# Two value banks in turn, and importance products moved to the end of a step, in a one-core decoder layer

## The chip, the cores and the metric

The kernel runs on one core of one Trainium2 chip. It is written engine by engine: TensorE does matrix products and full transposes and writes only to PSUM (8 banks of 512 float32 per partition), VectorE and ScalarE work element by element and read PSUM, GpSimd and SyncE do little here. The engines are held together by semaphores. The metric is the time on the device for one execution, in microseconds (us).

## The reference, cut to what matters

One decoder layer on 1024 tokens of width 1024: an input projection, then attention and a state-space mixer side by side, an output projection, and a mixture of experts. The change touches attention alone. Eight query heads share two key/value heads (four per group, `GQA`). For each block of 128 queries there are three branches, and their outputs are added with gates:

```python
p_cmp = masked_softmax(s, dist >= 0)                 # over 63 compressed keys
o_cmp = einsum('bkgqn,bnkd->bqkgd', p_cmp, v_cmp)
imp = einsum('bkgqn,nj->bkqj', p_cmp, ov)            # importance of 16 blocks of 64 keys
score = where(forced, FORCE_SCORE, where(valid, imp, -1.0))
_, idx = top_k(score, 8)                             # blocks that the selected branch may see
...                                                  # o_slc: softmax over the chosen blocks
...                                                  # o_win: softmax over the last 256 keys
o = gc[..., 0:1] * o_cmp + gc[..., 1:2] * o_slc + gc[..., 2:3] * o_win
```

Importance is needed only for query blocks 4 to 7: earlier blocks see at most 8 key blocks, so all are chosen.

## The kernel before

Attention (`attend`, L952) works through 24 groups, each a pair of branch and query block c: (CMP, 0), (WIN, 0), and then for each c (CMP, c+1), (WIN, c+1), (SEL, c). A group is cut into slots of some of the four heads per key/value head (`score_slots`): 46 slots (J) in all, one per group for CMP, two for most of WIN and for SEL 1 to 3, four for SEL 4 to 7. A slot is in flight over several steps, and each engine runs its own loop over steps j:

- TensorE (from L1223): scores of slot j; compressed values of slot j-2 (L1163, the products at L1170 for importance and L1175 for values) or values of slot j-2 (L1188), by kind; the turn of a finished group (L1198); transposes of the weights of slot j-1 (L1152), four 128 x 128 blocks to a PSUM bank, so one to four banks a slot; at times the transpose of a selection (L1205).
- ScalarE (from L1273): the copy of a finished group's values out of PSUM (`copy_values`, L1263), copies of the transposed weights of slot j-1 (L1270), exponentials of slot j (L1257).
- VectorE (from L1402): scores plus distance with the maximum (L1323), then `read_values` (L1327): the gates (L1337 to L1339), and either compressed values read straight from PSUM (L1343) and importance (L1347, then the release at L1350), or the turned values (L1353) and their addition (L1355); then the steps of the selection (L1365 to L1380) and the transposes of later queries (L293).

Values of WIN and SEL come out of the products with head width on the partitions and queries along the row; ScalarE copies them to SBUF and TensorE turns them with four transposes, so that VectorE can read them per query.

PSUM: scores use banks 0 to 3. All groups put their values into bank 6 (`O_BANK`). Transposes, importance, turned values, selections and one small product share banks 4, 5 and 7 in a fixed ring (`bank_users`, from L1059): the n-th user takes the bank of user n-3 and waits until that one has been read. Before the first products of a group, `bank_is_free` (L1155) waits for the reader of the group before: VectorE's read if it was CMP, ScalarE's copy if not. Each engine's order is fixed by its loop; an engine that waits holds up all that follows on it.

Of the kernel before, what the change touches and what calls it, by code (L numbers as in the profile page):

```python
# [24 lines left out]
P = 128  # L25
# [4 lines left out]
HD = 64  # L30
# [96 lines left out]
class Names:  # L127
# [11 lines left out]
    def sem(self, name):  # L139
        return self.stack.enter_context(self.nc.semaphore(name))  # L140
# [811 lines left out]
def attend(nc, N, M, A, C, out, next_tensor, next_vector):  # L952
# [20 lines left out]
    score_rows = M["score_rows"].rearrange("p (a c j) -> p a c j", a=2, c=NT)  # L973
    neg, coef, *den = (M["att_small"][:, i * 24:(i + 1) * 24].rearrange("p (b h) -> p b h", b=3) for i in range(4))
    o_T = M["misc"][:, 2048:3072].rearrange("p (b n) -> p b n", b=2)
    O_BANK, TURN_BANKS = 6, (4, 5, 7)

    gates_exp = sem("gates_exp")
    q_rows = M["q_rows"]
    scores_full, max_ready, exp_done = sem("scores_full"), sem("maxima_ready"), sem("exp_done")  # L980
    wT_full, wT_done = sem("weights_transposed"), sem("weightsT_copied")
    pv_done, o_read = sem("slot_values_done"), sem("values_read")
    oT_copied, o_turned, imp_read = sem("valuesT_copied"), sem("values_turned"), sem("importance_read")
    sel_ready, sel_full, sel_rows = sem("selection_ready"), sem("selection_transposed"), sem("selection_rows")
    prep_full, prep_steps = sem("ssd_constants_full"), sem("ssd_constants_steps")
    z_full, z_copied = sem("z_full"), sem("z_copied")
# [55 lines left out]
    def weightsT(j, k):  # L1042

        at = ((4096, 6144, 4608, 6656) if (J - 1 - j) % 2 == 0 else (0, 1024, 2048, 3072))[k]
        return M["big_u"][:, at:at + BANK]
# [10 lines left out]
    turns_before = lambda gi: sum(1 for x in turned if x < gi)  # L1056
    turn_at = {last_slot[groups[gi]] + 3: gi for gi in turned}
    imp_at = {last_slot[CMP, c] + 2: c for c in sel_count}
    bank_users, copy_use, sel_use, imp_use, turn_use, prep_use = [], [], {}, {}, {}, None  # L1059
    for j in range(J + 3):  # L1060
        if j in imp_at:
            imp_use[imp_at[j]] = len(bank_users)
            bank_users.append((imp_read, sel_count[imp_at[j]]))
        if j in turn_at:
            while j == J + 2 and TURN_BANKS[len(bank_users) % 3] != 7:
                bank_users.append(bank_users[-3])
            turn_use[turn_at[j]] = len(bank_users)
            bank_users.append((o_read, turn_at[j] + 1))
        if 1 <= j <= J:
            for k in range(len(banks_of(j - 1))):  # L1070
                copy_use.append(len(bank_users))
                bank_users.append((wT_done, len(copy_use)))
        if j in sel_at:
            sel_use[sel_at[j]] = len(bank_users)
            bank_users.append((sel_rows, sel_count[sel_at[j]]))
        if j == prep_at:
            prep_use = len(bank_users)
            bank_users.append((dt_sem, 7))
    bank_of = lambda use: TURN_BANKS[use % 3]

    queries_at = {0: [(1, 0), (1, 1)], 1: [(1, 2), (1, 3)]}
    for c in range(1, NT - 1):
# [26 lines left out]
    def tensor(pe):  # L1109
        def transpose_bank(use):  # L1110

            if use >= 3:
                pe.wait_ge(*bank_users[use - 3])
            return bank_of(use)

        def scores(j):
# [37 lines left out]

        def bank_is_free(gi):  # L1155

            if groups[gi - 1][0] == CMP:
                pe.wait_ge(o_read, gi)
            else:
                pe.wait_ge(oT_copied, turns_before(gi))  # L1160

        def compressed_values(j):

            gi, br, c, pairs = slots[j]
            pe.wait_ge(wT_done, copies_before[j + 1])
            rows = [weightsT(j, 0)[:, r * P:(r + 1) * P] for r in pairs]
            if c in sel_count:
                bank = transpose_bank(imp_use[c])
                for r in pairs:
                    nc.tensor.matmul(ps[:, bank, r * NG * N_BLK:(r + 1) * NG * N_BLK], rows[r], v_cmp[:, NG * HD:CMP_V],  # L1170
                                     start=True, stop=True)
            if gi >= 1:
                bank_is_free(gi)
            for r in pairs:
                last = nc.tensor.matmul(ps[:, O_BANK, r * P:(r + 1) * P], rows[r], v_cmp[:, 0:NG * HD], start=True, stop=True)  # L1175
            last.then_inc(pv_done, 1)

        def values(j):

            gi, br, c, pairs = slots[j]  # L1180
            if j == first_slot[br, c]:
                bank_is_free(gi)
            pe.wait_ge(wT_done, copies_before[j + 1])
            blocks, m = key_blocks(br, c), len(pairs)
            for b, blk in enumerate(blocks):
                for g in range(NG):
                    x = (b * NG + g) * m
                    last = nc.tensor.matmul(ps[g * HD:(g + 1) * HD, O_BANK, pairs[0] * P:(pairs[-1] + 1) * P],  # L1188
                                            vals[br][:, blk, g, 0:HD], weightsT(j, x // 4)[:, x % 4 * P:(x % 4 + m) * P],
                                            start=(b == 0), stop=(b == len(blocks) - 1))  # L1190
            last.then_inc(pv_done, 1)

        def turn_values(gi):

            pe.wait_ge(oT_copied, turns_before(gi) + 1)
            bank = transpose_bank(turn_use[gi])
            for r in range(GQ):
                last = nc.tensor.transpose(ps[:, bank, r * P:(r + 1) * P], o_T[:, turns_before(gi) % 2, r * P:(r + 1) * P],  # L1198
                                           ident[:, :])
            last.then_inc(o_turned, 1)  # L1200

# [21 lines left out]
        for j in range(J + 3):  # L1223
            n_t = len(banks_of(j - 1)) if 1 <= j <= J else 0
            if j < J:
                scores(j)
            if 2 <= j < J + 2 and slots[j - 2][1] == CMP:
                compressed_values(j - 2)
            if j in piece_at:
                z_pieces(piece_at[j][0], piece_at[j][1])  # L1230
            if j == J + 1:
                next_tensor(pe)
            if 2 <= j < J + 2 and slots[j - 2][1] != CMP:
                values(j - 2)
            if j in turn_at:
                turn_values(turn_at[j])
            if j in piece_at:
                z_pieces(piece_at[j][1], piece_at[j][2])
            for k in range(n_t):
                transposes(j - 1, k)  # L1240
            if j in sel_at:
                selection(sel_at[j])
            if j == prep_at:
                ssd_constants()

    def scalar(act):
# [13 lines left out]

        def copy_values(gi):
            act.wait_ge(pv_done, last_slot[groups[gi]] + 1)
            nc.scalar.activation(o_T[:, turns_before(gi) % 2, :], ps[:, O_BANK, :], ACT.Copy).then_inc(oT_copied, 1)  # L1263

        def copy_weights(j):
            for k, blocks in enumerate(banks_of(j)):
# [23 lines left out]
    def vector(dve):  # L1290
# [36 lines left out]
        def read_values(gi):  # L1327

            br, c = groups[gi]
            bank = O_BANK if br == CMP else bank_of(turn_use[gi])  # L1330
            O = ps[:, bank, :].rearrange("p (r g d) -> p g r d", r=GQ, g=NG)
            dst, tmp = by_head(o_att[:, c, :]), by_head(M["o_tmp"])
            gate_at = {CMP: 0, SEL: 1, WIN: 2}[br]
            d, f = (v[:, br, :] for v in (den[c % 2], coef))
            dve.wait_ge(exp_done, last_slot[br, c] + 1)
            if br == CMP:
                o.done(nc.vector.tensor_scalar(d, d, 1.0e-30, None, ALU.max))  # L1337
            o.done(nc.vector.reciprocal(d, d))
            o.done(nc.vector.tensor_tensor(f, d, sg[:, c, :, gate_at], ALU.mult))  # L1339
            fb = f.rearrange("p (g r) -> p g r", g=NG).unsqueeze(3).broadcast_to([P, NG, GQ, HD])  # L1340
            if br == CMP:
                dve.wait_ge(pv_done, last_slot[br, c] + 1)
                o.done(nc.vector.tensor_tensor(dst, O, fb, ALU.mult))  # L1343
                dve.sem_inc(o_read, 1)
                if c in sel_count:
                    imp_all = ps[:, bank_of(imp_use[c]), 0:GQ * NG * N_BLK].rearrange("p (r g j) -> p g r j", r=GQ, g=NG)
                    o.done(nc.vector.tensor_tensor(imp_h.rearrange("p (g r j) -> p g r j", g=NG, r=GQ), imp_all,  # L1347
                                                   d.rearrange("p (g r) -> p g r", g=NG).unsqueeze(3)
                                                   .broadcast_to([P, NG, GQ, N_BLK]), ALU.mult))
                    dve.sem_inc(imp_read, 1)  # L1350
            else:
                dve.wait_ge(o_turned, turns_before(gi) + 1)
                nc.vector.tensor_tensor(tmp, O, fb, ALU.mult).then_inc(o_read, 1)  # L1353
                dve.wait_ge(o_read, gi + 1)
                o.done(nc.vector.tensor_tensor(o_att[:, c, :], o_att[:, c, :], M["o_tmp"], ALU.add))  # L1355
                if gi == len(groups) - 1:
                    dve.sem_inc(rows_done, 1)

        def select(c, step):

# [39 lines left out]
        for gi, (br, c) in enumerate(groups):  # L1400
            read_at.setdefault(last_slot[br, c] + (2 if br == CMP else 3), []).append(gi)
        for j in range(J + 3):  # L1402
            if j < J:
                scores_with_distance(j)
            if j == 0:
# [1282 lines left out]
```

## Time and profile before

| | us |
|---|---|
| median of 3 runs | 1082.05 (1080.61 to 1083.12) |
| the profiled execution, its own time | 1081.66 |
| its span, first to last instruction | 1079.9 |
| TensorE busy | 1011.3 |
| VectorE busy | 645.8 |
| ScalarE busy | 345.6 |
| attention | about 305 to 605 us of the span |

Durations are those of one profiled execution. In the views PE is TensorE's matmul, PEld its weight load, DVE VectorE, ACT ScalarE. A row of the timeline merges neighbouring instructions of one line: start, duration of the row, engine, line, what it writes and reads, how many, and in brackets how long the engine was idle before and who released it. A row of a few matmuls ends a little later than the next row starts, as matmuls are pipelined. PEclk is the granted clock of TensorE: 1.00 is 2.4 GHz, 0.5 is 1.2 GHz, and a stretch between the two mixes them.

### The profile page before, as it was taken

To read this page: it belongs to the slowest core of one execution; us is meant where nothing else is said; L and a number is where in the kernel's file an instruction comes from. 1 tells how busy PE (TensorE), PEld (TensorE's weight loads), DVE (VectorE), ACT (ScalarE), POOL (GpSimd) and SP (SyncE) were. 2 spreads that over 40 slices of the span, in tenths; PEclk is the share of its full clock that TensorE was granted. 3 is DMA by queue.
4 is the path that set the end of the run, shared out by engine and by line. 5 is a ranking of instruction groups with operands and counts; after the bars stand their busy time and mean duration, and the time that the engine had idled before them with its cause. 6 is when DMAs were issued, how large, how long until landed. Compare 5 with 4: busy or idle time off the path is not lost.

```text
span 1079.9 us, 14099 instructions
## 1 busy us (share of the span) xinstructions
PE 1011.3 (94%) x4535; PEld 573.7 (53%) x4536; DVE 645.8 (60%) x1630; ACT 345.6 (32%) x974; POOL 175.4 (16%) x214
## 2 busy tenths in 40 slices
PE   8999999999998787878799899999989999999997
PEld 5544574444554554555556886555574444444443
DVE  3421222555254675676654598775577788887885
ACT  3311121121144665666666673322121000000000
POOL 0020131111000400000000210111012333333333
PEclk9999999999999988999999999999999999999999
DMA  7220042003000200000000501422749969999332
GB/s 267 90 71 0 1 81 78 21 17 103 1 1 1 79 1 1 1 1 2 1 1 2 188 9 34 157 77 99 252 152 319 351 228 332 327 385 350 126 115 95
DMA packets 73688, 119.26 MB, mean 110 GB/s; under 512 B 13888, under 2 KB 53152, under 8 KB 73632
## 3 DMA queue, kind: packets, MB, share of 16 engines
q1 hardware_dynamic: 62544, 87.59, 24.1%
q0 software_dynamic: 11088, 30.95, 8.1%
q8 instruction: 32, 0.52, 0.2%
q14 instruction: 24, 0.20, 0.1%
HBM read 105.41 MB, written 21.50 MB: 118 GB/s over the span
## 4 chain that ended last, share of the span: by engine, by line
PE 50%; ACT 10%; DVE 9%; issue 2%; DMA 0%; POOL 0%; DVEq 0%; POOLq 0%; ACTq 0%
PE ps L1858 16%; PE ps L1868 8%; ACT ring_gate_up L1257 5%; PE ps L2181 5%; PE ps L1188 4%; PE ps L1152 4%; PE ps L1218 3%; PE ps L1141 3%; ACT big_u L1270 3%; PE ps L2191 2%; PE ps L2212 1%; PE ps L1175 1%; PE ps L1198 1%; DVE big_u L2400 1%; ACT misc L1263 1%
## 5 line engine op out<-in xcount | busy, mean ns | idle before, releaser
L1672 DVE STREAM_TRANSPOSE big_w<-big_w 32x256 f32<-32x256 f32 x384 | 167.3, 436 | 28.3 <-DMA big_w<-hn_dram,misc 22.1
L1858 PE MATMUL ps<-ring_gate_up,big_w 128*128 (+1 forms) x400 | 179.8, 592 | 0.3 <-ACT big_w L1912 0.3
L519 PE MATMUL ps<-big_w,big_u 128*128 128x512 f32 (+1 forms) x448 | 174.6, 544 | 0.8 <-DVE big_u L795 0.8
L519 PEld LDWEIGHTS ps<-big_w,big_u 128*128 128x128 f32 x448 | 83.9, 192 | 77.3 <-issue 70.7
L1858 PEld LDWEIGHTS ps<-ring_gate_up,big_w 128*128 128x128 f32 x400 | 74.0, 190 | 83.8 <-issue 83.7
L1257 ACT ACTIVATE ring_gate_up<-ring_gate_up,big_w 128x64 f32<-128x64 f32 (+8 forms) x192 | 106.1, 562 | 1.1 <-DVE big_w L1323 1.1
L1323 DVE CUSTOM_DVE_ANT_0 ring_gate_up<-ps,ring_down 128x384 f32<-128x384 f32 (+7 forms) x128 | 73.9, 629 | 50.1 <-PE ps L1141 49.6
L1270 ACT ACTIVATE big_u<-ps 128x512 f32<-128x512 f32 (+1 forms) x126 | 66.4, 584 | 114.0 <-PE ps L1152 113.7
L1868 PE MATMUL ps<-ring_down,big_w 128*128 x200 | 90.0, 593 | 0.6 <-ACT big_w L1902 0.6
L1152 PE MATMUL ps<-ident,ring_gate_up 128*128 128x128 f32 x488 | 68.1, 287 | 17.1 <-DVEq L1350 12.7
L1188 PE MATMUL ps<-big_u,ring_down 128*64 128x128 f32 (+2 forms) x656 | 60.8, 331 | 17.7 <-ACT misc L1263 16.1
L1152 PEld LDWEIGHTS ps<-ident,ring_gate_up 128*128 128x128 f32 x488 | 57.1, 148 | 30.9 <-DVEq L1350 13.6
L1494 POOL TENSOR_SCALAR big_w<-big_w,vecT 128x1024 f32<-128x1024 f32 x8 | 23.2, 2907 | 251.1 <-DMA big_w<-in_w_out 251.1
L1141 PE MATMUL ps<-ring_down,misc 64*128 64x384 f32 (+3 forms) x320 | 63.1, 504 | 0.7 <-DVE big_w L1323 0.7
L1868 PEld LDWEIGHTS ps<-ring_down,big_w 128*128 128x128 f32 x200 | 37.9, 190 | 48.1 <-issue 48.1
L1902 ACT ACTIVATE big_w<-ps 128x256 f32<-128x256 f32 x25 | 9.6, 384 | 161.9 <-PE ps L1832 161.9
L1188 PEld LDWEIGHTS ps<-big_u,ring_down 128*64 128x64 f32 x656 | 38.8, 140 | 41.6 <-ACT misc L1263 19.1
L840 DVE TENSOR_REDUCE small<-ring_gate_up 128x2 f32<-128x128 f32 x16 | 4.6, 286 | 62.6 <-ACT ring_gate_up L659 42.4
L1795 POOL DMA_INDIRECT out<-big_u,misc x25 | 25.1, 1003 | 95.4 <-DVE big_u L1936 93.6
L293 DVE STREAM_TRANSPOSE misc<-ring_gate_up 32x128 f32<-32x128 f32 x128 | 38.7, 302 | 2.7 <-DVE ring_down L1343 0.2
L874 DVE TENSOR_TENSOR ring_gate_up<-ps,ring_gate_up 128x512 f32<-128x512 f32 x12 | 8.3, 693 | 52.9 <-PE ps L551 52.5
L1257 ACT ACTIVATION_READ_ACCUMULATOR ring_gate_up<-ring_gate_up,big_w 128x1 f32 x192 | 37.8, 197 | 0.0
(394 smaller groups left out, 1429.5 us busy)
## 6 DMA issues: line engine op xcount, KB each, us to landing
ring_gate_up<-in_w_gate SPq DMA_DIRECT2D x16, 1024.0 KB, 8.4
ring_gate_up<-in_w_up SPq DMA_DIRECT2D x16, 1024.0 KB, 12.4
ring_down<-in_w_down SPq DMA_DIRECT2D x16, 1024.0 KB, 14.3
misc<-in_x SPq DMA_DIRECT2D x16, 512.0 KB, 3.5
big_w<-in_w_in SPq DMA_DIRECT2D x6, 1024.0 KB, 7.0
big_w<-in_w_out SPq DMA_DIRECT2D x8, 512.0 KB, 5.1
hn_dram<-big_u SPq DMA_DIRECT2D x8, 512.0 KB, 2.6
out<-ring_gate_up SPq DMA_DIRECT2D x8, 512.0 KB, 3.9
```

What stands on the lines that cost most here:

```text
L293: last = nc.vector.transpose(dst[j * 32:(j + 1) * 32, :, i * 32:(i + 1) * 32], src[i * 32:(i + 1) * 32, :, d:d + 32])
L519: last = nc.tensor.matmul(ps[:, b, 0:width], uT[:, k, c * P:(c + 1) * P], wbuf[:, n % 2, k, 0:width], start=(k == 0), stop=(k == KD - 1))
L1141: last = nc.tensor.matmul(place(j, i, g)[:, at:at + w], Q[rows, c % 4, r * P:(r + 1) * P], rhs, start=not chosen, stop=True)
L1152: last = nc.tensor.transpose(ps[:, bank, i * P:(i + 1) * P], w_rows[:, at:at + P], ident[:, :])
L1188: last = nc.tensor.matmul(ps[g * HD:(g + 1) * HD, O_BANK, pairs[0] * P:(pairs[-1] + 1) * P], vals[br][:, blk, g, 0:HD], weightsT(j, x // 4 ...
L1257: last = nc.scalar.activation(w, w, ACT.Exp, bias=neg[:, br, h:h + 1], scale=-1.0, accum_out=den[c % 2][:, br, h:h + 1])
L1270: nc.scalar.activation(weightsT(j, k)[:, 0:w], ps[:, bank_of(copy_use[use]), 0:w], ACT.Copy).then_inc(wT_done, 1)
L1323: nc.vector.tensor_tensor_reduce(out=weights(j, i, g), in0=place(j, i, g), in1=table, scale=-SLOPES[h], scalar=1.0e20, op0=ALU.add, op1=AL ...
L1672: last = nc.vector.transpose(dst[j * 32:(j + 1) * 32, :, i * 32:(i + 1) * 32], src[i * 32:(i + 1) * 32, :, j * 32:(j + 1) * 32])
L1858: last = nc.tensor.matmul(ps[:, 2 + b, :], xT[:, b, k, :], ring_gu[:, bass.ds(at + k * 2 * D_EXP, BANK)], start=(k == 0), stop=(k == KD - 1))
L1868: last = nc.tensor.matmul(ps[:, 4 + 2 * b + half, :], hT[:, b, f, :], ring_d[:, bass.ds(at + f * D + half * BANK, BANK)], start=(f == 0), ...
L2181: last = nc.tensor.matmul(ps[:, bank, :], left[:, k, :], right[:, k, :], start=(k == 0 and starts), stop=(k == 3), skip_group_check=True)
```

## The change

Groups put their values into banks 6 and 7 in turn, by their number. A group may start when the group two before it has been read. The turned values go back into the bank that they came from. The ring for transposes, importance and selection has two banks, 4 and 5, and a user waits for the one two before. The importance products leave `compressed_values`, where they stood ahead of the compressed values, and come after the transposes of the same step; VectorE reads them at the start of the next step, ahead of its scores.

```diff
-    O_BANK, TURN_BANKS = 6, (4, 5, 7)
+    o_bank = lambda gi: 6 + gi % 2
...
-    bank_of = lambda use: TURN_BANKS[use % 3]
+    bank_of = lambda use: 4 + use % 2
...
-            if use >= 3:
-                pe.wait_ge(*bank_users[use - 3])
+            if use >= 2:
+                pe.wait_ge(*bank_users[use - 2])
             return bank_of(use)
...
         def bank_is_free(gi):
 
-            if groups[gi - 1][0] == CMP:
-                pe.wait_ge(o_read, gi)
-            else:
-                pe.wait_ge(oT_copied, turns_before(gi))
+            if gi >= 2:
+                pe.wait_ge(o_read, gi - 1)
...
-            if c in sel_count:
-                bank = transpose_bank(imp_use[c])
-                for r in pairs:
-                    nc.tensor.matmul(ps[:, bank, r * NG * N_BLK:(r + 1) * NG * N_BLK], rows[r], v_cmp[:, NG * HD:CMP_V],
-                                     start=True, stop=True)
-            if gi >= 1:
-                bank_is_free(gi)
+            bank_is_free(gi)
...
+        def importance(c):
+            j = last_slot[CMP, c]
+            bank = transpose_bank(imp_use[c])
+            for r in slots[j][3]:
+                last = nc.tensor.matmul(ps[:, bank, r * NG * N_BLK:(r + 1) * NG * N_BLK], weightsT(j, 0)[:, r * P:(r + 1) * P],
+                                        v_cmp[:, NG * HD:CMP_V], start=True, stop=True)
+            last.then_inc(imp_steps, 1)
...
             pe.wait_ge(oT_copied, turns_before(gi) + 1)
-            bank = transpose_bank(turn_use[gi])
             for r in range(GQ):
-                last = nc.tensor.transpose(ps[:, bank, r * P:(r + 1) * P], o_T[:, turns_before(gi) % 2, r * P:(r + 1) * P],
+                last = nc.tensor.transpose(ps[:, o_bank(gi), r * P:(r + 1) * P], o_T[:, turns_before(gi) % 2, r * P:(r + 1) * P],
                                            ident[:, :])
...
             for k in range(n_t):
                 transposes(j - 1, k)
+            if j in imp_at:
+                importance(imp_at[j])
...
+        def read_importance(c):
+            imp_all = ps[:, bank_of(imp_use[c]), 0:GQ * NG * N_BLK].rearrange("p (r g j) -> p g r j", r=GQ, g=NG)
+            dve.wait_ge(imp_steps, 2 * sel_count[c] - 1)
+            nc.vector.tensor_tensor(imp_h.rearrange("p (g r j) -> p g r j", g=NG, r=GQ), imp_all,
+                                    den[c % 2][:, CMP, :].rearrange("p (g r) -> p g r", g=NG).unsqueeze(3)
+                                    .broadcast_to([P, NG, GQ, N_BLK]), ALU.mult).then_inc(imp_steps, 1)
+            dve.wait_ge(imp_steps, 2 * sel_count[c])
...
         for j in range(J + 3):
+            if j - 1 in imp_at:
+                read_importance(imp_at[j - 1])
             if j < J:
                 scores_with_distance(j)
```

## Rows read from the trace of the kernel before

**Rows 1.** The page: busy time, share of the span, instructions.
```profile
PE 1011.3 (94%) x4535; PEld 573.7 (53%) x4536; DVE 645.8 (60%) x1630; ACT 345.6 (32%) x974; POOL 175.4 (16%) x214
```
**Rows 2.** Stretches of the attention stage: length, busy of each engine, clock, DMA.
```profile
305.00:350.00 45.00, 41.56 (x207) 22.70 (x206) 22.26 (x124) 18.65 (x75) 0.00 (x0) 0.96 0.00 1
350.00:400.00 50.00, 39.06 (x252) 27.00 (x254) 34.11 (x131) 34.09 (x113) 11.84 (x5) 0.90 0.12 43
400.00:450.00 50.00, 39.12 (x258) 25.62 (x256) 28.43 (x111) 30.07 (x90) 0.00 (x0) 0.86 0.00 1
450.00:500.00 50.00, 38.31 (x338) 27.02 (x334) 37.08 (x131) 30.52 (x95) 0.00 (x0) 1.00 0.01 1
500.00:550.00 50.00, 43.73 (x370) 29.31 (x371) 29.39 (x90) 33.00 (x86) 0.00 (x0) 0.97 0.00 1
```
**Rows 3.** Waits from 305 to 612 us: total, times, longest.
```profile
PE ps L1188 <- ACT misc L1263: 16.1, 8, 3.1
...
PE ps L1152 <- DVEq L1350: 12.7, 4, 3.6
...
PE ps L1175 <- ACT misc L1263: 10.1, 7, 2.2
...
PE ps L1141 <- DVE big_w L1323: 2.0, 4, 0.9
...
PE ps L1188 <- DVEq L1344: 0.8, 2, 0.6
```
**Rows 4.** Timeline of TensorE: first value products of a group.
```profile
355.41 1.08 PE L1188 MATMUL ps<-big_u,ring_down 128*64 128x512 f32 x4 [2.36 <-ACT misc L1263]
...
377.35 1.08 PE L1188 MATMUL ps<-big_u,ring_down 128*64 128x256 f32 x8 [2.13 <-ACT misc L1263]
...
406.80 2.83 PE L1188 MATMUL ps<-big_u,ring_down 128*64 128x256 f32 x12 [3.14 <-ACT misc L1263]
...
442.91 3.13 PE L1188 MATMUL ps<-big_u,ring_down 128*64 128x256 f32 x16 [3.05 <-ACT misc L1263]
...
475.66 1.31 PE L1188 MATMUL ps<-big_u,ring_down 128*64 128x128 f32 x20 [1.38 <-ACT misc L1263]
...
579.65 1.97 PE L1188 MATMUL ps<-big_u,ring_down 128*64 128x128 f32 x32 [1.29 <-ACT misc L1263]
```
**Rows 5.** Timeline of TensorE: compressed values in steps without importance.
```profile
329.70 1.13 PE L1175 MATMUL ps<-big_w,big_u 128*128 128x128 f32 x8 [2.15 <-ACT misc L1263]
...
361.16 1.65 PE L1175 MATMUL ps<-big_w,big_u 128*128 128x128 f32 x8 [2.16 <-ACT misc L1263]
```
**Rows 6.** Timeline of TensorE: a step with importance.
```profile
492.95 1.08 PE L1170 MATMUL ps<-big_w,big_u 128*128 128x32 f32 x8
495.03 1.16 PE L1175 MATMUL ps<-big_w,big_u 128*128 128x128 f32 x8 [1.00 <-ACT misc L1263]
...
500.07 1.09 PE L1152 MATMUL ps<-ident,ring_gate_up 128*128 128x128 f32 x8 [3.01 <-DVEq L1350]
```
**Rows 7.** Timeline of VectorE in the same step.
```profile
498.83 0.69 DVE L1343 TENSOR_TENSOR ring_down<-ps,big_w 128x512 f32<-128x512 f32 x1
499.66 0.29 DVE L1347 TENSOR_TENSOR big_w<-ps,big_w 128x128 f32<-128x128 f32 x1
```
**Rows 8.** Timeline of TensorE and ScalarE: transposes and copies of four-bank slots.
```profile
574.11 2.00 PE L1152 MATMUL ps<-ident,ring_gate_up 128*128 128x128 f32 x16
...
574.80 2.06 ACT L1270 ACTIVATE big_u<-ps 128x512 f32<-128x512 f32 x4 [1.54 <-PE ps L1152]
...
574.80 0.60 ACT L1270 ACTIVATE big_u<-ps 128x512 f32<-128x512 f32 x1 [1.54 <-PE ps L1152]
...
588.92 2.07 ACT L1270 ACTIVATE big_u<-ps 128x512 f32<-128x512 f32 x4 [1.84 <-PE ps L1152]
...
591.04 1.97 PE L1188 MATMUL ps<-big_u,ring_down 128*64 128x128 f32 x32 [0.81 <-ACT big_u L1270]
```

More of the change, by code:

```diff
@@ L982, in attend @@
     pv_done, o_read = sem("slot_values_done"), sem("values_read")
-    oT_copied, o_turned, imp_read = sem("valuesT_copied"), sem("values_turned"), sem("importance_read")
+    oT_copied, o_turned = sem("valuesT_copied"), sem("values_turned")
+    imp_steps = sem("importance_full_then_read")
     sel_ready, sel_full, sel_rows = sem("selection_ready"), sem("selection_transposed"), sem("selection_rows")
@@ L1058, in attend @@
     imp_at = {last_slot[CMP, c] + 2: c for c in sel_count}
[L1059 to L1068, printed above, removed]
+    bank_users, copy_use, sel_use, imp_use, prep_use = [], [], {}, {}, None
+    for j in range(J + 2):
         if 1 <= j <= J:
@@ L1072, in attend @@
                 bank_users.append((wT_done, len(copy_use)))
+        if j in imp_at:
+            imp_use[imp_at[j]] = len(bank_users)
+            bank_users.append((imp_steps, 2 * sel_count[imp_at[j]]))
         if j in sel_at:
@@ L1166, in compressed_values @@
             rows = [weightsT(j, 0)[:, r * P:(r + 1) * P] for r in pairs]
-            if c in sel_count:
-                bank = transpose_bank(imp_use[c])
-                for r in pairs:
-                    nc.tensor.matmul(ps[:, bank, r * NG * N_BLK:(r + 1) * NG * N_BLK], rows[r], v_cmp[:, NG * HD:CMP_V],
-                                     start=True, stop=True)
-            if gi >= 1:
-                bank_is_free(gi)
+            bank_is_free(gi)
             for r in pairs:
-                last = nc.tensor.matmul(ps[:, O_BANK, r * P:(r + 1) * P], rows[r], v_cmp[:, 0:NG * HD], start=True, stop=True)
+                last = nc.tensor.matmul(ps[:, o_bank(gi), r * P:(r + 1) * P], rows[r], v_cmp[:, 0:NG * HD], start=True, stop=True)
             last.then_inc(pv_done, 1)
@@ L1187, in values @@
                     x = (b * NG + g) * m
-                    last = nc.tensor.matmul(ps[g * HD:(g + 1) * HD, O_BANK, pairs[0] * P:(pairs[-1] + 1) * P],
+                    last = nc.tensor.matmul(ps[g * HD:(g + 1) * HD, o_bank(gi), pairs[0] * P:(pairs[-1] + 1) * P],
                                             vals[br][:, blk, g, 0:HD], weightsT(j, x // 4)[:, x % 4 * P:(x % 4 + m) * P],
@@ L1240, in tensor @@
                 transposes(j - 1, k)
+            if j in imp_at:
+                importance(imp_at[j])
             if j in sel_at:
@@ L1262, in copy_values @@
             act.wait_ge(pv_done, last_slot[groups[gi]] + 1)
-            nc.scalar.activation(o_T[:, turns_before(gi) % 2, :], ps[:, O_BANK, :], ACT.Copy).then_inc(oT_copied, 1)
+            nc.scalar.activation(o_T[:, turns_before(gi) % 2, :], ps[:, o_bank(gi), :], ACT.Copy).then_inc(oT_copied, 1)
         def copy_weights(j):
@@ L1329, in read_values @@
             br, c = groups[gi]
-            bank = O_BANK if br == CMP else bank_of(turn_use[gi])
-            O = ps[:, bank, :].rearrange("p (r g d) -> p g r d", r=GQ, g=NG)
+            O = ps[:, o_bank(gi), :].rearrange("p (r g d) -> p g r d", r=GQ, g=NG)
             dst, tmp = by_head(o_att[:, c, :]), by_head(M["o_tmp"])
@@ L1344, in read_values @@
                 dve.sem_inc(o_read, 1)
[L1345 to L1350, printed above, removed]
             else:
```

## The prediction

> **What bounds the kernel now.** First the page: TensorE is busy for 94% of the span [rows 1], so what can be won is its idle time and its slow time. Then the table of stretches, because that share is an average: before 305 us TensorE is nearly full, and in the attention stage (305 to 605 us, the only stage that is edited) it is busy for 38 to 44 us of each 50, and its granted clock falls to 0.96, 0.90, 0.86, then 1.00 and 0.97 [rows 2]. Third, the waits of that stage, which name who was waited for. Four of them concern the edit: the value products at L1188 wait 16.1 us for ScalarE's copy of the previous group's values (L1263), the compressed values at L1175 wait 10.1 us for the same copy, the weight transposes at L1152 wait 12.7 us for VectorE's release of the importance bank (L1350), and L1188 waits 0.8 us for VectorE's read of compressed values (L1344) [rows 3]. They sum to 39.7 us. Last, the timeline around single waits, which shows what could run in their place.
>
> The stage is a ring: ScalarE ends the exponentials of a slot, TensorE transposes its weights, ScalarE copies them and starts the next exponentials. At a change of group, two more links are put in: ScalarE's copy of the old values, and TensorE's first products of the new group, which stand ahead of the turn of the old values and of the transposes. Nothing outside the stage is needed to pass a gain on: the next stage starts from its last row, and TensorE bounds what follows.
>
> **1. Values no longer wait for the old group's copy.** The new group has the other bank, so its products run while ScalarE still copies; the turn comes behind them and still waits for the copy. So a wait is not lost whole: it shrinks by the length of the products that now lie in it, or goes if they are longer. For the eight changes to a WIN or SEL group the waits are 2.36, 2.13, 3.14, 3.05, then four of 1.38, 1.38, 1.35 and 1.29 (six of the eight stand in [rows 4]). The products last (start to the next instruction's start, at the full clock) about 1.0, 1.0, 1.45, 1.9, and from 1.25 to 1.9 for the other four. Saved: 1.0 + 1.0 + 1.45 + 1.9 + 1.25 + 1.38 + 1.35 + 1.29 = 10.6 us. For compressed groups without importance there are three waits of 2.15 to 2.16 us (two of them in [rows 5]), with 1.0 us of products to put in. In the first, z products stand between as well and fill it: 2.15; the other two give 1.0 each. Together 4.2 us. In the four compressed steps with importance the products of importance already ran ahead of the wait (1.08 us, then 1.00 us idle [rows 6]); now the compressed products take their place, and the rest of the wait stays: 0 saved here.
>
> The new wait in `bank_is_free` is for the read of group gi-2. It is tightest where a one-slot compressed group lies between: SEL c-1, CMP c+1, WIN c+1. VectorE reads SEL before CMP in the same step, and before the change WIN waited for the later one, so this wait is met by at least the length of that later read, 0.69 us [rows 7], earlier; the 0.8 us of L1344 go. Behind it TensorE has only its own queue. The price of an unmet wait there would be some tenths, four to eight times; I take 0. The in-place turn writes a bank that its own copy has left: no new wait, and the use of a ring bank goes.
>
> **2. Importance at the end of the step.** Before, its bank was one of three in the ring, and the second bank of transposes of the same step needed it back, which took the whole of VectorE's reads: in the step at 492.95 the transposes stop for 3.01 us until L1347 has ended at 499.95 [rows 6, 7]. Four such waits, 12.7 us. Now the products come behind the last transposes and the bank is next wanted in the following step, behind the next scores and behind value products of 1 us and more [rows 4]; VectorE reads it first thing in that step, 0.29 us [rows 7]. Its next scores are not there before TensorE has done them after the importance products, so what is queued behind this read (maxima, then exponentials) waits for nothing more. If that cover were gone, it is 0.3 to 0.5 us, four times: 2 us. I take 12.7 us saved. The products themselves change place, not number.
>
> **3. Two ring banks for three.** This is the cost. Slots of WIN from c=2 and of SEL from c=2 need 3 or 4 banks of transposes: 32 of the 46 slots. The third bank now waits until ScalarE has copied the first. In a step of four banks, transposes start at 574.11 and take 0.49 us a bank (16 in 2.00), ScalarE's first copy starts at 574.80 and lasts 0.60, so the first bank is free at 575.40. TensorE resumed 0.05 us after such a copy (copies end at 590.99, product at 591.04) [rows 8]. The third bank starts at 575.45 and not at 575.08: 0.37 us. The fourth then needs the second copy, ended at 575.89, and is due at 575.94: nothing more. ScalarE's third copy shifts with it, so its exponentials do too, and both sides of the ring are late by 0.37. 32 x 0.37 = 11.8 us; where TensorE waits for VectorE's maxima instead (four times, 2.0 us [rows 3]) it is hidden, so I take 11. Bounds: 0 if all of it fell into other waits, and, if each extra bank (22 slots with one, 10 with two: 42) paid the whole of fill and copy, 0.69 + 0.60 + 0.05 - 0.49 = 0.85 us each, 36 us.
>
> **4. The clock.** In the five stretches the clock below 1 stands for 1.8 + 5.0 + 7.0 + 0 + 1.5 = 15.3 us; by TensorE's busy share (0.8) some 12 us of work lost [rows 2]. It shows in durations: eight compressed products take 1.65 us at 361.16 and 1.16 at 495.03 [rows 5, 6], and sixteen values products 3.13 at 442.91 [rows 4]. The slow stretches follow waits of 2.1 to 3.1 us; behind the four waits of about 1.3 us the clock stayed. After the change the longest wait left is 3.14 - 1.45 = 1.7 us, the others 1.3 or less. I take three quarters of 12: 9 us. Bounds: 0 and 13.
>
> Sum: 10.6 + 4.2 + 0.8 + 12.7 - 11 + 9 = 26.3 us. The profiled execution took 1081.66 us (span 1079.9), which gives 1055.4; the median of the runs is 0.4 higher: **1056 us**.
>
> **Rivals.**
> A. The clock doesn't come back (other idle time of the same sum takes its place). For it: even 2.15 us waits were enough. Then 1082 - 17.3 = 1065 us.
> B. The copy bounds anyway, so a second values bank gives nothing, and only 12.7 saved against 11 to 12 paid is left: 1081 us. For it: the turn still waits for the same copy. Against it: the products now stand ahead of that copy's end, and ScalarE sits idle before the transposes reach it even in slots without a change of group, 1.54 and 1.84 us [rows 8].
> C. The ring of two banks runs in turns rather than overlapped. The mechanism is the 0.85 us per extra bank above: 36 us against 28.3 saved, no clock back: 1089 us, slower. It decides from 28.3 / 42 = 0.67 us per extra bank on. Against it: ScalarE is idle before the first copy of a slot [rows 8], since transposes start only when its exponentials are done, so it takes each bank at once.
> D. The short stops of part 3 pull the clock down where it is full now. If 450 to 605 us ran at 0.86 as 400 to 450 does [rows 2], that is 155 us by 0.12 of clock by a busy share of 0.87, 16 us lost, with none regained: 1082 - 17 + 16 = 1081 us. Against it: the late slots had stops of 1.3 us [rows 4] at a nearly full clock.
> The Trainium skill, page TensorE: Matmul & The Clock Gate, section on psum-queue depth-cycling, warns of just this: cycling through PSUM banks leaves TensorE idle for short moments and its clock swings. By that rule D would hold; the trace so far has no two-bank ring to show it.
> The same page, in its section on HAM oscillation, reports a kernel to which double-buffered PSUM gave nothing more. By that rule the outcome would be B's. Here L1188 and L1175 do wait for a bank, 26.2 us in all [rows 3], so I give it little.
>
> **How the numbers follow.** Forecast 0.64; A 0.20; B 0.06; C 0.05; D 0.05. The forecast's own spread: stalls of 0.25 to 0.5 us (8 to 16 us), clock 5 to 13 us, the saved waits 25 to 30 us: 1047 to 1064. With A's side the range is 1046 to 1072. About 0.2% (2 us) is what a measurement of this kernel tells from no change. Faster by more: forecast, A and a part of B, 0.86; within: most of B and D, 0.06; slower: C and what of B and D falls beyond 2 us, 0.08.
>
> **What would show it.** Right: no wait of L1175 or L1188 for L1263, which moves to L1198 with some 8 to 10 us in total; none of L1152 for L1350; a new wait of L1152 for ScalarE's copies L1270, about 30 times 0.37 us; copies of a four-bank slot last about 2.4 us for 2.06; clock at 0.97 or more in all stretches; the stage ends some 26 us earlier, and the stages behind it last as long as before. Wrong: the wait for L1270 is over 0.67 us each (C), the clock falls behind 450 us (D), L1198 takes over the whole 26 us (B), or VectorE's maxima wait in the step after importance.

## The result, and the profile after

The changed kernel takes 1050.86 us (median of 4, 1049.57 to 1050.92), the kernel before 1082.59 (4, 1080.61 to 1083.2) beside it: ratio 0.9707, 95% interval 0.969 to 0.9724. That is 31.7 us less, where 26.3 were forecast; the time lies inside the range of 1046 to 1072. The span of the profiled execution fell from 1079.9 to 1049.1 us, 30.8 us. The first product of the next stage (L1502) moved from 595.13 to 565.49 us, 29.6 us earlier, so the gain arises inside the attention stage and is passed on whole. From its first score product (299.52 us before, 299.76 after) to that point the stage is 29.9 us shorter.

The table of stretches of the kernel after (length, busy of PE, PEld, DVE, ACT and POOL, PEclk, DMA) answers to [rows 2]:

```profile
305.00:350.00 45.00, 43.25 (x227) 23.83 (x226) 23.82 (x129) 22.04 (x88) 0.53 (x1) 1.00 0.04 11
350.00:400.00 50.00, 40.64 (x304) 26.59 (x304) 37.32 (x155) 38.78 (x123) 11.33 (x4) 1.00 0.09 34
400.00:450.00 50.00, 44.82 (x329) 28.66 (x327) 41.39 (x143) 37.40 (x112) 0.00 (x0) 1.00 0.00 1
450.00:500.00 50.00, 45.68 (x431) 32.36 (x429) 35.61 (x122) 35.72 (x92) 0.00 (x0) 1.00 0.01 2
500.00:550.00 50.00, 46.44 (x406) 30.47 (x404) 27.92 (x65) 35.52 (x87) 0.00 (x0) 1.00 0.01 1
```

The clock is 1.00 in all five, where it was 0.96, 0.90, 0.86, 1.00 and 0.97. Only from 550 to 605 us does it read 0.94, behind the 2.06 us wait at the head of the next stage (L1507), which both kernels have; before, this lay just past 604 us. The waits from 300 to 582 us (total, times, longest) answer to [rows 3]; L1193 is the turn, L1148 the transposes, L1260 and L1267 ScalarE's copies of values and of weights, L1254 its exponentials:

```profile
PE ps L1193 <- ACT misc L1260: 11.3, 11, 1.6
PE ps L1148 <- ACT big_u L1267: 8.0, 32, 0.3
PE ps L1148 <- ACT ring_gate_up L1254: 4.6, 7, 1.7
...
PE ps L1137 <- DVE big_w L1320: 0.7, 1, 0.7
```

The waits of values and compressed values for the copy, and the wait of transposes for the release of importance, are gone. What is left stands at the turn, and the ring of two banks has its 32 stops. A group of 12 value products with the turn behind it shows how the wait shrank: before, 3.14 us of idle time stood ahead of the products at 406.80 [rows 4]; now the turn waits 1.61 us behind them.

```profile
393.51 1.52 PE L1176 MATMUL ps<-big_u,ring_down 128*64 128x256 f32 x12
396.63 0.66 PE L1193 MATMUL ps<-ident,misc 128*128 128x128 f32 x4 [1.61 <-ACT misc L1260]
```

The step with importance, TensorE's timeline, answers to [rows 6]: compressed values, turn, two banks of transposes, the third after its stop, then importance (L1185).

```profile
468.58 1.16 PE L1163 MATMUL ps<-big_w,big_u 128*128 128x128 f32 x8
470.66 0.66 PE L1193 MATMUL ps<-ident,misc 128*128 128x128 f32 x4 [0.92 <-ACT misc L1260]
471.15 1.04 PE L1148 MATMUL ps<-ident,ring_gate_up 128*128 128x128 f32 x8
472.44 0.66 PE L1148 MATMUL ps<-ident,ring_gate_up 128*128 128x128 f32 x4 [0.25 <-ACT big_u L1267]
472.93 1.07 PE L1185 MATMUL ps<-big_w,big_u 128*128 128x32 f32 x8
```

VectorE's timeline just behind it: the read of importance, and then 1.24 us in which it waits for the next scores. So the read delays nothing, as the prediction assumed.

```profile
474.36 0.29 DVE L1352 TENSOR_TENSOR big_w<-ps,big_w 128x128 f32<-128x128 f32 x1
475.88 0.96 DVE L1320 CUSTOM_DVE_ANT_0 ring_gate_up<-ps,ring_down 128x768 f32<-128x768 f32 x1 [1.24 <-PE ps L1137]
```

A four-bank slot, TensorE and ScalarE, answers to [rows 8]: the third bank starts 1.29 us behind the first (0.97 without the stop), so the stop costs 0.32 us from start to start; ScalarE's four copies last from 551.86 to 554.29, 2.43 us for 2.06, 0.37 us more. There is one stop in the slot, not two.

```profile
551.22 1.04 PE L1148 MATMUL ps<-ident,ring_gate_up 128*128 128x128 f32 x8
552.51 1.15 PE L1148 MATMUL ps<-ident,ring_gate_up 128*128 128x128 f32 x8 [0.25 <-ACT big_u L1267]
...
551.86 1.09 ACT L1267 ACTIVATE big_u<-ps 128x512 f32<-128x512 f32 x2 [1.83 <-PE ps L1148]
553.20 1.09 ACT L1267 ACTIVATE big_u<-ps 128x512 f32<-128x512 f32 x2 [0.26 <-PE ps L1148]
```

### The profile page after: what moved, and what is told of

Read it like the earlier page. It is cut to its first block, busy times and chain, and to the rows that moved or that the text cites. A ratio compares the mean times of both kernels' runs of the same rounds, so it can differ in the third digit from the quotient of the medians.

```text
span 1049.1 us, 14082 instructions
## 1 busy us (share of the span) xinstructions
PE 1002.5 (96%) x4535; PEld 565.1 (54%) x4536; DVE 644.1 (61%) x1630; ACT 347.9 (33%) x974; POOL 175.2 (17%) x214
## 4 chain that ended last, share of the span: by engine, by line
PE 51%; ACT 9%; DVE 8%; issue 2%; DMA 0%; POOL 0%; POOLq 0%; DVEq 0%; ACTq 0%
PE ps L1858 16%; PE ps L1868 8%; PE ps L2181 5%; ACT ring_gate_up L1254 5%; PE ps L1148 4%; PE ps L1137 3%; PE ps L1176 3%; ACT big_u L1267 3%; PE ps L1213 3%; PE ps L2191 2%; PE ps L2212 1%; DVE big_u L2400 1%; PE ps L1193 1%; DVE ring_down L2522 1%; PE ps L1131 1%
## 5 line engine op out<-in xcount | busy, mean ns | idle before, releaser
L1254 ACT ACTIVATE ring_gate_up<-ring_gate_up,big_w 128x64 f32<-128x64 f32 (+8 forms) x192 | 105.8, 556 | 1.1 <-DVE big_w L1320 1.1
L1267 ACT ACTIVATE big_u<-ps 128x512 f32<-128x512 f32 (+1 forms) x126 | 68.3, 582 | 81.8 <-PE ps L1148 81.7
L1148 PE MATMUL ps<-ident,ring_gate_up 128*128 128x128 f32 x488 | 69.8, 280 | 13.1 <-ACT big_u L1267 8.0
L1148 PEld LDWEIGHTS ps<-ident,ring_gate_up 128*128 128x128 f32 x488 | 52.8, 141 | 32.8 <-ACT big_u L1267 15.6
L1137 PE MATMUL ps<-ring_down,misc 64*128 64x384 f32 (+3 forms) x320 | 59.8, 482 | 0.2
L1176 PE MATMUL ps<-big_u,ring_down 128*64 128x128 f32 (+2 forms) x656 | 57.9, 320 | 0.7 <-ACT big_u L1267 0.7
L1254 ACT ACTIVATION_READ_ACCUMULATOR ring_gate_up<-ring_gate_up,big_w 128x1 f32 x192 | 36.7, 191 | 0.0
## 6 DMA issues: line engine op xcount, KB each, us to landing
ring_gate_up<-in_w_up SPq DMA_DIRECT2D x16, 1024.0 KB, 12.6
ring_down<-in_w_down SPq DMA_DIRECT2D x16, 1024.0 KB, 14.6
```

The lines of the kernel that those rows point to most:

```text
L1137: last = nc.tensor.matmul(place(j, i, g)[:, at:at + w], Q[rows, c % 4, r * P:(r + 1) * P], rhs, start=not chosen, stop=True)
L1148: last = nc.tensor.transpose(ps[:, bank, i * P:(i + 1) * P], w_rows[:, at:at + P], ident[:, :])
L1176: last = nc.tensor.matmul(ps[g * HD:(g + 1) * HD, o_bank(gi), pairs[0] * P:(pairs[-1] + 1) * P], vals[br][:, blk, g, 0:HD], weightsT(j, x ...
L1254: last = nc.scalar.activation(w, w, ACT.Exp, bias=neg[:, br, h:h + 1], scale=-1.0, accum_out=den[c % 2][:, br, h:h + 1])
L1267: nc.scalar.activation(weightsT(j, k)[:, 0:w], ps[:, bank_of(copy_use[use]), 0:w], ACT.Copy).then_inc(wT_done, 1)
```

## The experiments

All are compared with runs of the kernel before on the same chip (medians 1082.6 to 1083.4 us).

**One half alone: importance.**

```diff
 (kernel before)
-            if c in sel_count:
-                bank = transpose_bank(imp_use[c])
...
             for k in range(n_t):
                 transposes(j - 1, k)
+            if j in imp_at:
+                importance(imp_at[j])
...
+            if j - 1 in imp_at:
+                read_importance(imp_at[j - 1])
```

> Only one half of the change: the importance products stand behind the transposes and are read first in the next step; values stay in bank 6 and the ring keeps three banks. My theory (the gains of the two halves help each other): the four waits for the release of importance, 12.7 us, go, but the compressed products now wait for ScalarE's copy without importance products lying in that wait, which gives 4 x 1.05 = 4.2 us back; the clock regains some 3 us after those waits only. 1082.6 - 12.7 + 4.2 - 3 = 1071 us (1067 to 1075). If the halves were independent (rival), it gives the whole 12.7 and the clock: 1066 us or less.

Measured: 1067.6 us, ratio 0.9853 (0.9819 to 0.9886), 12 to 20 us saved. The waits for the copy of values (L1269) of this kernel, at values and at compressed values:

```profile
PE ps L1184 <- ACT misc L1269: 15.4, 8, 3.1
PE ps L1171 <- ACT misc L1269: 14.5, 7, 2.2
```

Compressed values now wait 14.5 us where they waited 10.1: the 4.4 us that importance products had filled are back, as expected. The time alone does not exclude the rival (1066 or less); this row does. The granted clock was 0.98, 0.95, 0.90, 1.00 and 0.97 in the five stretches. If (1 - clock) times the length of each stretch is summed, that is 9.9 us of low clock instead of 15.3. Counted in full it gives 12.7 - 4.4 + 5.4 = 13.7 us, and at 0.8 of it (the busy share of the prediction) 12.6; both are inside the interval.

**The other half alone: value banks and the ring of two.**

```diff
 (changed kernel)
+            if c in sel_count:
+                bank = transpose_bank(imp_use[c])
...
             bank_is_free(gi)
...
-            if j in imp_at:
-                importance(imp_at[j])
```

> Only the other half: values in banks 6 and 7 in turn, turned in place, ring of two banks; importance stays ahead of the compressed values and is read behind them. My theory: the waits for the copy shrink by 14.8 us and by 4 more, since importance and compressed products now both lie in the wait; L1344's 0.8 us go; two ring banks cost 0.37 us in 28 steps (in the four importance steps the wait for its release hides it), 10.4 us; the slow clock between 350 and 450 us mostly comes back, 8 to 10 us, but that after the four long waits stays. 1082.6 - 19.6 + 10.4 - 9 = 1064 us (1060 to 1069). Rival (the second values bank gives nothing, the copy bounds anyway): 1082 + 10 = 1093 us.

Measured: 1066.22 us, ratio 0.9832 (0.9796 to 0.9868). Its waits:

```profile
PE ps L1148 <- DVEq L1341: 12.7, 4, 3.6
PE ps L1148 <- ACT big_u L1262: 7.0, 28, 0.3
PE ps L1190 <- ACT misc L1255: 6.4, 6, 1.6
```

The waits for the copy fell from 26.9 to 6.4 us, 28 stops came, and the 12.7 us for the release of importance stand untouched. A second values bank does give something: the rival of 1093 is out. The clock came back in part: 0.99 from 350 to 400 us, but 0.86 again from 400 to 450, where two of the four long waits lie. The halves' gains add to 34 us with 4 us of uncertainty on each; whether they help or hinder each other in time can't be told from 31.7.

**The price alone: a ring of two, turned values in bank 7.**

```diff
 (kernel before)
-    O_BANK, TURN_BANKS = 6, (4, 5, 7)
+    O_BANK, TURN_BANK = 6, 7
-    bank_of = lambda use: TURN_BANKS[use % 3]
+    bank_of = lambda use: 4 + use % 2
```

> The kernel before with the price alone: transposes, importance and selections in a ring of two banks (4, 5), turned values in bank 7 for themselves, values in bank 6 as before. My theory: a stall of 0.37 us on the third bank in 28 steps outside the importance steps: +10.4 us, less where the transposes run at the low clock (their pitch then hides it): 1090 to 1093 us, 1092. Rival (the stall falls into other waits): within 2 us of 1082.6. Rival (ring in turns, 0.85 us for each of 42 extra banks): over 1110 us.

Measured: 1091.49 us, ratio 1.0074 (1.0048 to 1.01), 5 to 11 us slower, with 1092 forecast: the price is that of one stop a step, and not 0.85 us for each extra bank. Its wait of transposes for ScalarE's copies:

```profile
PE ps L1147 <- ACT big_u L1267: 6.5, 26, 0.3
```

Its 8 runs show besides how time and clock go together: 1087.62 us at a mean clock of 0.984, 1092.57 at 0.976, 1097.1 at 0.973. A straight line through all 8 gives 0.7 us for each 0.001 of clock, and one through the 17 runs of the kernel before gives the same. Counted in full, 0.001 of 1090 us would be 1.1 us, so some two thirds of it show in the time.

**The clock alone: idle time filled, no wait removed.**

```diff
 (kernel before)
+        def fill(bank, n):
+            for _ in range(n):
+                nc.tensor.matmul(ps[:, bank, 0:P], ones, ones, start=True, stop=True)
...
+                    fill(transpose_bank(turn_use[gi - 1]), 20 if c in (2, 3) else 12 if c < 2 else 6)
                 bank_is_free(gi)
...
+                if j in imp_at and k == 1:
+                    pe.wait_ge(max_ready, heads_before[j + 1])
+                    fill(0, 20)
                 transposes(j - 1, k)
```

> The kernel before with idle time filled and no wait removed: dummy 128x128 products of ones, whose result is never read, ahead of TensorE's wait for the copy of values (6 to 20 of them, into the bank of the coming turn) and, in the four importance steps, 20 of them ahead of the second bank of transposes (into bank 0, after all maxima). Theory (a slow clock after long idle cost some 13 us, and shrinking the waits gave it back): the clock reads 0.98 or more in every stretch and the time falls by 10 to 14 us, to 1069 to 1073 us, though nothing else is changed. Rival (the low clock costs little on the path, and the 5 us beyond my forecast are from elsewhere): 1082 us, or more by what the dummies overrun.

Measured: 1078.2 us, ratio 0.9957 (0.9937 to 0.9977). The clock was 1.00 in each of the five stretches, but only 5 us came of it. The timeline says why: 20 dummies are 40 instructions that last 4.7 us together, and the values behind them start at 405.74 though ScalarE's copy had ended at 404.24.

```profile
401.07 4.73 PE L1118 MATMUL ps<-ones 128*128 128x128 f32 x40
405.74 1.52 PE L1196 MATMUL ps<-big_u,ring_down 128*64 128x256 f32 x12
...
403.66 0.58 ACT L1274 ACTIVATE misc<-ps 128x512 f32<-128x512 f32 x1
```

So the same with 8, 12, 5 and 12 dummies in place of 12, 20, 6 and 20:

> The filled kernel with fewer dummies. Each float32 dummy took two passes, 0.23 us, so 20 took 4.6 us and overran waits of 3.1 us by 1.5 us, those of 2.1 us by 0.6, of 1.3 us by 0.1, in all some 12 us. Now 8, 12, 5 and 12 of them (1.9, 2.8, 1.15 and 2.8 us), each inside its wait. If the slow clock was worth the 14 us that the change gained beyond its waits: clock still at 0.99 or more in every stretch and 1083 - 13 = 1070 us (1067 to 1073). If it is worth the 5 us that the first filled kernel showed: 1078 us again.

Measured: 1068.81 us, ratio 0.9862 (0.9843 to 0.9881): 13 to 17 us. Values are still held up by copies and transposes by importance, only with work in most of that time; the two stretches that were lowest (0.90 and 0.86) now read:

```profile
350.00:400.00 50.00, 45.96 (x352) 32.51 (x352) 34.87 (x137) 36.70 (x121) 11.86 (x5) 1.00 0.12 43
400.00:450.00 50.00, 46.61 (x359) 33.75 (x356) 35.07 (x135) 33.72 (x107) 0.00 (x0) 1.00 0.00 1
```

Over the stage, from the first score product to the first product of the next stage, the two profiled executions compare like this, the kernel before first:

```profile
299.52 1.11 PE L1141 MATMUL ps<-big_w,misc 64*128 64x64 f32 x16 [0.74 <-PEq L385]
...
595.13 0.60 PE L1502 MATMUL ps<-ident,ring_gate_up 128*128 128x128 f32 x4
```
```profile
301.50 1.11 PE L1145 MATMUL ps<-big_w,misc 64*128 64x64 f32 x16 [0.74 <-PEq L385]
...
584.15 0.60 PE L1513 MATMUL ps<-ident,ring_gate_up 128*128 128x128 f32 x4
```

The stage is 13.0 us shorter (282.65 for 295.61), with the clock at 1.00 in all five stretches. This is the cleanest measure of the term that I sized too small: 13.0 us where the stretches had 15.3 us of low clock, so 0.85 of it. The medians differ by more, 14.6 us: the profiled execution of the kernel before had a mean clock of 0.982, its 7 runs beside this kernel one of 0.978.

**The turn ahead of the value products.**

```diff
 (changed kernel)
+            if j in turn_at:
+                turn_values(turn_at[j])
             if 2 <= j < J + 2 and slots[j - 2][1] == CMP:
                 compressed_values(j - 2)
...
-            if j in turn_at:
-                turn_values(turn_at[j])
```

> The changed kernel, but the turn of a finished group stands ahead of the next group's value products and not behind them; two value banks stay. It takes away what lies in the wait for the copy and nothing else. My theory (the gain of the second values bank is only that products lie in this wait): the 15.6 us are lost again, and with waits of 2 to 3 us back, part of the clock: 1050.9 + 15.6 + 0 to 9 = 1066 to 1076 us. Rival (the copy and the turn bound anyway; the gain of the second bank came from elsewhere, such as no wait for VectorE's reads): within 3 us of 1051.

Measured: 1078.71 us, ratio 0.9962 (0.9945 to 0.9979): some 28 us of the 31.7 are lost by the place of four transposes (the turn) alone. Its wait, and one of its steps:

```profile
PE ps L1193 <- ACT misc L1260: 30.2, 16, 3.1
```
```profile
406.61 1.11 PE L1193 MATMUL ps<-ident,misc 128*128 128x128 f32 x4 [3.05 <-ACT misc L1260]
407.65 2.83 PE L1176 MATMUL ps<-big_u,ring_down 128*64 128x256 f32 x12
```

18.9 us are longer waits (30.2 for 11.3); I had expected 15.6 and forgot the importance products, which no longer lie in four of them. The other 9 us go with the clock, 0.96, 0.93, 0.86 and 0.93 up to 500 us: the products behind the wait take 2.83 us where they take 1.52 at the full clock. The time lies above my range (1066 to 1076): the waits are 3.3 us more than I had, and the clock stands at the upper end of the 0 to 9 us that I gave it.

**The turn behind the second bank of transposes.**

```diff
 (changed kernel)
             for k in range(n_t):
                 transposes(j - 1, k)
+                if k == min(1, n_t - 1) and j in turn_at:
+                    turn_values(turn_at[j])
```

> The changed kernel with the turn moved behind the second bank of transposes of its step (behind the first where there is only one). The transposes need the exponentials, which ScalarE ends before it starts the copy of values, so they can run while it copies; and the turn (0.49 us) fills the 0.37 us in which the third bank waits. My theory: ScalarE's first copy of weights follows its copy of values at once, so each of 11 changes of group that still wait gains about 1.0 us, the four late ones 0.3: 1050.9 - 12 = 1039 us (1037 to 1044). Rival: VectorE reads the turned values 0.4 us later in each of these steps and its reads, selection and query transposes are then what the next scores wait for: 1048 to 1052 us.

Measured: 1050.2 us, ratio 0.9704 (0.9677 to 0.9731), no gain over the changed kernel. The wait for the copy is gone but for 0.7 us, and another has its place: scores (L1137) wait for VectorE's maxima.

```profile
PE ps L1137 <- DVE big_w L1322: 10.0, 9, 2.3
```

The 1039 us of my theory are out, and the rival was right. The clock was lower too: 0.987 to 0.992 over its runs, where all runs of the changed kernel had 0.996.

**Value products held back for the third bank.**

```diff
 (changed kernel)
+            hold = 2 if j + 2 < J + 1 and len(banks_of(j + 1)) > 2 and len(blocks) > 1 else 0
+            todo = todo[:len(todo) - hold] if part == 0 else todo[len(todo) - hold:]
...
                 transposes(j - 1, k)
+                if k == 1 and n_t > 2 and 2 <= j < J + 2 and slots[j - 2][1] != CMP:
+                    values(j - 2, 1)
```

> The changed kernel with the last two value products of a slot held back and put between the second and third bank of transposes (steps with 3 or 4 banks). They take about 0.12 to 0.25 us and fill the stall of TensorE. Theory 1 (in the late slots TensorE is the bound, and the stall costs TensorE's time): 20 steps by 0.15 to 0.25 us, 1047 us (1045.5 to 1048.5). Theory 2 (the stall costs because ScalarE's third copy is late, TensorE's time doesn't count): no change, 1051 us.

Measured: 1051.03 us, ratio 0.971 (0.9683 to 0.9737): no change. The stops fell from 8.0 to 1.5 us, and 3.5 us of it went into longer waits for ScalarE (7.0 for 4.6 and 12.4 for 11.3):

```profile
PE ps L1197 <- ACT misc L1266: 12.4, 11, 2.0
PE ps L1148 <- ACT ring_gate_up L1260: 7.0, 10, 1.8
...
PE ps L1148 <- ACT big_u L1273: 1.5, 6, 0.3
```

So in part the second theory. The other 3 us should have shown. The clock of its runs was 0.991 to 0.995 for 0.996, and at 0.7 us for each 0.001 that would be 1 to 4 us, but this is argued and not tested.

**Both, and the turn behind the first bank.** The kernel with the turn behind the second bank and held products in steps without a turn:

> Both of the two edits before: the turn between the banks of transposes, and two value products held back in steps without a turn. If both gains hold and touch different steps, they add: 1039 - 3 = 1036 us. If the ring is bound by ScalarE once the turn is out of its way, holding products back gives nothing more: as the kernel with the turn moved alone.

Measured: 1044.86 us (1042.61 to 1046.14), ratio 0.9662 (0.9635 to 0.9688), far from the 1036 that both gains would have given. It is 5 us below the kernel with the turn moved alone, but the two intervals overlap. The stops of the transposes for ScalarE's copies no longer stand among its waits; the longest in total are those for maxima (L1328) and for exponentials (L1262):

```profile
PE ps L1137 <- DVE big_w L1328: 9.4, 9, 1.7
PE ps L1148 <- ACT ring_gate_up L1262: 8.7, 14, 1.7
```

Why two moves that gave nothing each should give 5 us together stays open. Then the turn behind the first bank (`k == 0` for `k == min(1, n_t - 1)`), alone and with held products:

> The changed kernel with the turn behind the first bank of transposes and not the second. The turn then begins when the copy of values ends, 0.05 us behind it, as in the changed kernel, so VectorE has the turned values no later; ScalarE has its first bank 0.6 us or more sooner, and the turn fills the third bank's stall. Theory (behind the second bank it was VectorE, 0.4 us later, that took the gain): 11 changes of group by 0.6 to 0.75 us and four by 0.3: 1050.9 - 9 = 1042 us (1040 to 1046). Rival (VectorE's path from maxima over reads to maxima is the bound at a change of group in any case): 1050 us.

> That, and the last two value products held back behind the second bank in the steps without a turn. Held products gained nothing alone and some 5 us beside the turn behind the second bank. If this gain is TensorE's stall time in the late slots, it adds here too: 1042 - 4 = 1038 us. If it came only from the clock of that run: 1042 us.

Measured: 1047.96 us, ratio 0.9679 (0.9662 to 0.9696), and 1046.08 us, ratio 0.9655 (0.9639 to 0.9672). With the turn alone behind the first bank, the wait for maxima is about half as long, though not gone:

```profile
PE ps L1148 <- ACT ring_gate_up L1256: 8.6, 15, 1.7
PE ps L1137 <- DVE big_w L1322: 5.6, 7, 1.6
```

The turn alone gave 3 us of the 9 expected, and the held products 2 of the 4 expected; neither step is clear of noise by itself, as the intervals overlap. The last kernel (0.9639 to 0.9672) is clear of the changed one (0.969 to 0.9724). So, by a hair, is the one with the turn behind the second bank and held products (0.9688), whose median is the lowest; the two can't be told apart.

## Why the prediction was right

**Values bank (15.6 us forecast with L1344's 0.8).** Right in mechanism and size. Waits for the copy fell from 26.9 us (16.1, 10.1 and 0.7 at the last turn) to 11.3, so 15.6 us, where 14.8 were forecast, and L1344's 0.8 went. What is left stands at the turn, 11.3 us where 8 to 10 were forecast. That figure was a slip: the prediction's own terms leave 26.2 - 14.8 = 11.4 us, of which the four steps with importance keep 0.76 to 0.97 us each, and the last turn adds 0.7. The kernel with the turn first shows the reason: take the products out of the wait and the gain is gone. Rival B falls with it. The Trainium skill, page TensorE: Matmul & The Clock Gate, section on HAM oscillation, reports a kernel that gained nothing more from double-buffered PSUM. That does not carry over: the half with the value banks gave 14 to 22 us here.

**Importance (12.7 us).** Right: 12.7 us to 0, and its read ahead of the scores is covered. Alone it gives back 4.4 us at the compressed values; I had that only for the sum of both.

**The ring of two (11 us).** Right: 32 stops, as counted, of 0.25 us of idle time each (8.0 us in all) and not the 0.37 forecast; the 0.37 is there in the copies of a four-bank slot, 2.43 us for a forecast 2.4. The price measured by itself is 5 to 11 us. Rival C's 36 us are out.

**The clock (9 us).** The term that was mis-sized. By the table of stretches the low clock stood for 15.3 us; I multiplied by the busy share (12 us) and then took three quarters. All of it went: 1.00 in every stretch. The waits account for 15.6 + 0.8 + 12.7 - 11.8 = 17.3 of the 29.9 us of the stage (the ring at its forecast 32 x 0.37), so 12.6 are left for the clock, and filling the idle time alone gave 13.0. The three quarters, for which the prediction gives no reason, were the error. The busy share was not: 15.3 us of low clock cost 13.0, which is 0.85, and over the runs of one program it is some two thirds. With 13 in place of 9 the sum is 30.3 and the time 1051.8 us.

My reading of what brings the clock down was also too simple. I wrote that the slow stretches follow waits of 2.1 to 3.1 us. The longest wait of the kernel before, 3.64 us for the release of importance, left no trace in the clock: the transposes behind it take 1.09 us, and 450 to 500 us reads 1.00.

```profile
462.29 1.09 PE L1152 MATMUL ps<-ident,ring_gate_up 128*128 128x128 f32 x8 [3.64 <-DVEq L1350]
```

With the value banks alone the same wait of 3.64 us, at 444.27, is followed by transposes of 1.97 us. So a long wait can bring the low clock and need not; which one does, no run here settles. The range has a slip too: with every term at its worst the forecast's own spread ends at 1068 us and not at 1064, still inside the 1072 of the range.

**Rivals A and D.** A (the clock doesn't come back) was given 0.20; the five rows at 1.00 rule it out. For D stood the Trainium skill, same page, section on psum-queue depth-cycling: cycling through PSUM banks makes the clock swing. In the changed kernel it doesn't: 32 stops, clock at 1.00. In the ring of two alone, beside the long waits, the clock was 0.973 to 0.985 over 8 runs, 0.979 in the mean, and 0.974 to 0.982 over the 17 runs of the kernel before, with the same mean. Its profiled execution has 0.93 and 0.94 from 450 to 550 us for 1.00 and 0.97 before, but over the runs no effect shows.

## What to carry to other kernels

A second bank gains as much as the work that comes to lie in the wait, so place ready work ahead of the waiting instruction: the whole change gained 4 us with the four waiting transposes ahead of the value products, and 32 us with them behind. Where long waits and a low granted clock stand in the same stretches, count the low clock beside the waits, scaled by TensorE's busy share and not discounted again; dummy products that fit inside the waits measure it by itself. And when one wait is cut, read who is second: here it was VectorE's maxima and ScalarE's exponentials, and further moves, though they took the wait for the copy away, gave 6 us at most.

## What the runs showed of the hardware

Granted clock differs between executions of one program: 0.973 to 0.985 for the ring of two, with 9.5 us between its ends, but 0.996 in all four runs of the changed kernel, whose longest wait between 350 and 560 us is 1.6 us. A wait of 2.3 us for VectorE, in the kernel with the turn behind the second bank, came with low clock right behind it (scores of 1.13 us took 2.05); one of 3.64 us in the kernel before did not. A float32 product of 128 x 128 shows as two instructions of 0.12 us each (40 in 4.73 us), which is what spoiled the first filled kernel.
